# Ten retention query and key tiles moved to the seven-product pairs, with their rotation done per chunk on GpSimd

## What is computed

```python
proj = h @ w_in[l]
(c_q, c_kv, k_pe, gate_mla, q_ret, k_ret, v_ret, gate_ret,
 merge_mla, merge_ret) = jnp.split(proj, pts, axis=-1)
y_mla = mla_branch(...) * jax.nn.silu(gate_mla)            # 8 heads, causal softmax
y_ret = retention_branch(q_ret, k_ret, v_ret, positions, g_ret[l]) * jax.nn.silu(gate_ret)
merged = (jax.nn.sigmoid(merge_mla) * (y_mla @ w_proj_mla[l])
          + jax.nn.sigmoid(merge_ret) * (y_ret @ w_proj_ret[l]))
x = x + gate * (merged @ w_out[l])                         # then a final rmsnorm
```

```python
inner = (q k^T * decay) v        # within a chunk
cross = (q R) * xi               # with the state R of the chunks before
R = R * gamma_c + (k * zeta)^T v
```

## Time and profile before

| | |
|---|---|
| median of 3 runs | 1627.0 us (1626.59 to 1627.08) |
| the profiled execution: its time | 1629.6 us |
| its span, first to last instruction | 1627.8 us |
| PE busy | 1581.9 us, 97% of the span |
| DVE busy | 985.8 us, 61% |
| ACT busy | 579.9 us, 36% |
| POOL busy | 233.7 us, 14% |
| granted TensorE clock | 0.995 of full speed |
| instructions | 20108 |

### The profile page before, as it was taken

The page is one execution under the profiler, slowest core; times in us unless marked ns, Lnnn a source line. Parts: engine busy times, 40 slices in busy tenths (PEclk is TensorE's granted clock), DMA queues, the critical chain, the costliest instruction groups (busy, mean ns, idle before and its releaser), DMA issues.

```text
span 1627.8 us, 20108 instructions
## 1 busy us (share of the span) xinstructions
PE 1581.9 (97%) x7660; PEld 1320.8 (81%) x7660; DVE 985.8 (61%) x1576; ACT 579.9 (36%) x984; POOL 233.7 (14%) x180
## 2 busy tenths in 40 slices
PE   5999999999999999999999999999999999999998
PEld 4778888888888888888888878888788888888886
DVE  6984444444447957656665555657877775547544
ACT  5444333333334323332343333334543333213111
POOL 2232223323211212112000000001101000000000
PEclk9999999999999999999999999999999999999999
DMA  9132232233241576777655465537987877335322
GB/s 387 34 129 104 110 110 110 111 117 116 103 141 45 153 288 234 287 269 265 218 188 179 155 205 168 194 130 229 360 257 246 263 236 277 124 125 199 135 103 78
DMA packets 150991, 292.31 MB, mean 180 GB/s; under 512 B 10736, under 2 KB 91504, under 8 KB 142960
## 3 DMA queue, kind: packets, MB, share of 16 engines
q1 hardware_dynamic: 132816, 253.47, 45.0%
q10 hardware_dynamic: 13472, 20.78, 4.0%
q0 software_dynamic: 4608, 16.78, 2.6%
HBM read 187.71 MB, written 102.76 MB: 178 GB/s over the span
## 4 chain that ended last, share of the span: by engine, by line
PE 82%; DVE 10%; DMA 3%; ACT 3%; issue 1%; POOL 1%; SPq 0%; DVEq 0%; ACTq 0%
PE p_banks L2050 8%; PE p_banks L2008 8%; PE p_banks L2011 8%; PE p_banks L2010 8%; PE p_banks L1923 4%; PE p_banks L1925 4%; PE p_banks L1924 4%; PE p_banks L2082 4%; PE p_banks L2257 4%; PE p_banks L2256 4%; PE p_banks L2258 4%; PE p_banks L2315 2%; PE p_banks L2316 2%; PE p_banks L2317 2%; DMA w_raw<-in_w_dense 2%; PE p_banks L2149 2%
## 5 line engine op out<-in xcount | busy, mean ns | idle before, releaser
L1518 DVE TENSOR_TENSOR w_form<-w_pair,w_form 128x512 fp32r<-128x512 f32 x120 | 92.9, 776 | 101.8 <-ACT w_form L1172 100.5
L1172 ACT ACTIVATE w_form<-w_pair 128x512 fp32r<-128x512 f32 x120 | 75.6, 632 | 195.4 <-PE p_banks L2011 187.3
L519 ACT ACTIVATE w_hi<-w_raw 128x1024 fp32r<-128x1024 f32 (+3 forms) x79 | 70.1, 889 | 202.4 <-PE p_banks L2258 99.5
L1923 PE MATMUL p_banks<-h_hi,w_hi 128*128 128x512 f32 x304 | 118.6, 390 | 2.0 <-DVE w_lo L525 1.6
L1924 PE MATMUL p_banks<-h_lo,w_hi 128*128 128x512 f32 x304 | 118.4, 389 | 0.0
L1925 PE MATMUL p_banks<-h_hi,w_lo 128*128 128x512 f32 x304 | 118.3, 389 | 0.0
L525 DVE TENSOR_TENSOR w_lo<-w_raw,w_hi 128x1024 fp32r<-128x1024 f32 (+3 forms) x80 | 92.3, 1158 | 28.6 <-ACT w_hi L519 28.3
L1242 ACT ACTIVATE prob<-p_banks,neg_max 128x128 f32<-128x128 f32 (+3 forms) x64 | 47.5, 742 | 163.8 <-DVE neg_max L1621 163.8
L2258 PE MATMUL p_banks<-y_hi,w_lo 128*128 128x512 f32 x256 | 99.6, 389 | 0.0
L2257 PE MATMUL p_banks<-y_lo,w_hi 128*128 128x512 f32 x256 | 99.6, 389 | 0.0
L2256 PE MATMUL p_banks<-y_hi,w_hi 128*128 128x512 f32 x256 | 99.6, 389 | 0.0
(11 more groups left out here) (291 smaller groups left out, 4255.2 us busy)
## 6 DMA issues: line engine op xcount, KB each, us to landing
w_raw<-in_w_dense SPq DMA_DIRECT2D x45, 512.0 KB, 5.6
w_pair<-in_w_pairs SPq DMA_DIRECT2D x20, 1024.0 KB, 4.9
v_ret<-v_stage POOLq DMA_DIRECT2D x32, 512.0 KB, 4.1
qk_chunk<-qk_chunks SPq DMA_DIRECT2D x32, 512.0 KB, 4.4
v_chunk<-v_ret SPq DMA_DIRECT2D x32, 512.0 KB, 5.0
qk_chunks<-split_stage SPq DMA_DIRECT2D x28, 512.0 KB, 6.0
merge_t<-act_t SPq DMA_DIRECT2D x48, 256.0 KB, 3.4
act_t<-stage SPq DMA_DIRECT2D x40, 256.0 KB, 2.0
```

What stands on the lines that cost most here:

```text
L1518: nc.vector.tensor_tensor(self.form[f % FORM_SLOTS][:, 1, :], self.form_source(f), self.form[f % FORM_SLOTS][:, 0, :].bitcast(F32), ALU.su ...
L1923: nc.tensor.matmul(out, w_hi[:, slot, cut], x_hi[:, k, tok], start=(k == ks[0]), stop=False)
```

## The change

It does six things.

1. The first ten of the 16 retention query and key tiles (heads 0 and 1, and the queries of head 2) leave `SEQ` and form five more pairs (25 instead of 20). Six "x" tiles stay, three ahead of "q" 0 and three behind "v" 3; between them no "x" stands any more.
2. None of the 16 is rotated or split there. Their half tiles (pairs) or tiles (x) are copied by ACT and stored as plain float32 in chunk order, in pieces of 512 B. The scratch tensor `qk` has half its size.
3. In retention, a chunk's four raw tiles (256 KB) and its cosine and sine (128 KB, 512 B pieces) are loaded two chunks ahead into two slots. POOL rotates them with four instructions (`rotate_chunk`), ACT writes the high parts (`high_qk`) and DVE the low parts (`low_qk`). POOL's key sums go.
4. The norming of the latents is spread over the three first "x" tiles instead of six.
5. In attention, ACT's exp and DVE's reciprocal and scaling of a step stand ahead of the eviction of filled tiles instead of behind it.
6. In the last output tile, the left half's final scaling is done by ACT, beside DVE's of the right half, and its product with `g_final` is taken earlier.

```diff
+GATES = 16
+RAW, RAW_FIRST = 6, 3
...
-SEQ += [("x", n) for n in range(6)]
-SEQ += [("q", 0), ("q", 1), ("q", 2), ("q", 3), ("a", 0), ("b", 0), ("x", 6), ("q", 4), ("q", 5), ("x", 7),
-        ("q", 6), ("q", 7), ("a", 1), ("b", 1), ("x", 8), ("k", 0), ("k", 1), ("k", 2), ("k", 3), ("x", 9)]
+SEQ += [("x", n) for n in range(RAW_FIRST)]
+SEQ += [("q", 0), ("q", 1), ("q", 2), ("q", 3), ("a", 0), ("b", 0), ("q", 4), ("q", 5), ("q", 6), ("q", 7),
+        ("a", 1), ("b", 1), ("k", 0), ("k", 1), ("k", 2), ("k", 3)]
 for n in range(4):
-    SEQ += [("k", 4 + n), ("v", n)] + [("x", 10 + n)] * (n < 2)
-SEQ += [("x", n) for n in range(12, TURNS)]
+    SEQ += [("k", 4 + n), ("v", n)]
+SEQ += [("x", n) for n in range(RAW_FIRST, RAW)]
...
-PAIRS = ACT_TILES // 2
+GATE_PAIRS = ACT_TILES // 2
+PAIRS = GATE_PAIRS + (4 * H_RET - RAW) // 2
...
     def load_qk_chunk(self, sp, n):
-        if n >= 3:
-            sp.wait_ge(self.out_done, n - 2)
-        sp.dma_start(self.qk[:, n % 3, :, :].rearrange("p c n -> p (c n)").bitcast(F32), self.d["qk"][n // NT, n % NT])\
-            .then_inc(self.chunk_loaded[n % 3], 16)
+        if n >= 2:
+            sp.wait_ge(self.k_turned, n - 1)
+            sp.wait_ge(self.qk_lo_ready, n - 1)
+        h, m = divmod(n, NT)
+        sp.dma_start(self.qk_raw[:, n % 2, 0:4, :].rearrange("p c n -> p (c n)"), self.d["qk"][h, m])\
+            .then_inc(self.chunk_loaded[n % 2], 16)
+        sp.dma_start(self.qk_raw[:, n % 2, 4:6, :], self.d["ret_tables"].rearrange("a p n -> p a n")[:, :, m * P:(m + 1) * P])\
+            .then_inc(self.chunk_loaded[n % 2], 16)
...
         for n in range(CHUNK_STEPS):
+            if n + 2 < CHUNK_STEPS:
+                self.load_qk_chunk(sp, n + 2)
             if n + 3 < CHUNK_STEPS:
-                self.load_qk_chunk(sp, n + 3)
                 self.load_v_chunk(sp, n + 3)
...
+    def rotate_chunk(self, pool, n):
+
+        raw, late = self.qk_raw[:, n % 2, :, :], int(n >= 6)
+        by_sine = self.by_sine[late]
+        cos, sin = (raw[:, c:c + 1, :].broadcast_to([P, 4, P]) for c in (4, 5))
+        pool.wait_ge(self.chunk_loaded[n % 2], 32 * (n // 2 + 1))
...
+        if n:
+            pool.wait_ge(self.qk_step, 4 * n)
+        self.nc.gpsimd.tensor_tensor(by_sine[:, :, :], raw[:, 0:4, :], sin, ALU.mult).then_inc(self.qk_step, 1)
+        pool.wait_ge(self.qk_step, 4 * n + 1)
+        self.nc.gpsimd.tensor_tensor(raw[:, 0:4, :], raw[:, 0:4, :], cos, ALU.mult).then_inc(self.qk_step, 1)
+        pool.wait_ge(self.qk_step, 4 * n + 2)
+        self.nc.gpsimd.tensor_tensor(raw[:, 0:2, :], raw[:, 0:2, :], by_sine[:, 2:4, :], ALU.subtract).then_inc(self.qk_step, 1)
+        self.nc.gpsimd.tensor_tensor(raw[:, 2:4, :], raw[:, 2:4, :], by_sine[:, 0:2, :], ALU.add).then_inc(self.qk_step, 1)
...
+    def high_qk(self, act, n):
+        act.wait_ge(self.qk_step, 4 * n + 4)
+        if n >= 2:
+            act.wait_ge(self.out_done, n - 1)
+        self.nc.scalar.activation(self.qk[:, n % 2, 0:4, :], self.qk_raw[:, n % 2, 0:4, :], ACT.Copy).then_inc(self.qk_hi_ready, 1)
+
+    def low_qk(self, dve, n):
+        dve.wait_ge(self.qk_hi_ready, n + 1)
+        self.nc.vector.tensor_tensor(self.qk[:, n % 2, 4:8, :], self.qk_raw[:, n % 2, 0:4, :],
+                                     self.qk[:, n % 2, 0:4, :].bitcast(F32), ALU.subtract).then_inc(self.qk_lo_ready, 1)
...
             nc.vector.tensor_tensor(self.y_ret[:, s, :, :], p[:, 0, :].rearrange("p (a n) -> p a n", n=P),
                                     self.gate_chunk[:, n % 3, :, :], ALU.mult).then_inc(self.yr_done, 1)
+            if n + 2 < CHUNK_STEPS:
+                self.low_qk(dve, n + 2)
...
     def turn_keys(self, pe, n):
-        pe.wait_ge(self.k_summed, n + 1)
+        pe.wait_ge(self.qk_step, 4 * n + 4)
...
     def inner_scores(self, pe, n):
-        pe.wait_ge(self.chunk_loaded[n % 3], 16 * (n // 3 + 1))
+        pe.wait_ge(self.qk_lo_ready, n + 1)
```

262 lines of the change are left out of this document (141 added, 121 removed).

## The result

| | before | after |
|---|---|---|
| median | 1627.04 us (1626.59 to 1627.25, 4 executions) | 1679.70 us (1676.73 to 1680.08, 4 executions) |
| ratio, 95% interval | | 1.032 [1.0302, 1.0338] |
| span of the profiled execution | 1627.8 us | 1678.2 us |
| PE busy | 1581.9 us | 1587.8 us |
| POOL busy | 233.7 us | 322.9 us |

The change costs 52.7 us. The forecast was 1651, +24, with a range up to 1680: the sign and the place were right, the size was less than half of it.

The account below looks back on a forecast made before the run. PE, busy for 97% of the span, was taken to bound the kernel. 1629.6 - 13.6 + 38 + 3 - 3 - 0.6 = 1653.4; with the median 2.6 under the profiled execution, the forecast was 1651, range 1612 to 1680.

Parts of the forecast that it names:

- Fewer matmuls, -13.6: Pairs and sequence: five new pairs save 60 matmuls at 0.227 us each, all on the path, 13.6 us.
- the sequence, +3: Sequence: loads and stores of the unbroken "q" to "v" tiles make PE wait, +3 us, ends 0 and +12.
- The third rival: Sequence starves: loads and stores lag from k0 to v3, PE loses 12 us, total 1626, no difference; chance 0.05.
- Attention, -3: Attention: with exp ahead of evictions, PE's 4.3 us wait for exp shrinks, -3 us, ends 0 and -6.
- Retention, +38: Retention: the late-load rotation loop takes 17.6 us for two chunks, 8.8 a chunk against 7.54, times 30, +38 us.
- bn_stats to the end of `y_ret` (5.35 + 0.5): Retention loop: DVE's 5.35 us to the gated output, plus 0.5 us for POOL being in DVE's way, ends 0 and 2.6.
- The 0.15 taken off for chunks without a state: Retention loop: chunks at a head's end have no state, lowering the two-chunk sum from 17.75 to 17.6 us.
- The 0.5 us added to POOL's fourth instruction: Retention rotation: the fourth instruction stands straight behind another and takes longer, raising POOL's 4.1 us to 4.6.
- Hidden rotation: Retention: rival that the two-chunk loop takes no more than 15.1 us, total 1610, faster; chance 0.14.
- The case in which both DVE instructions wait at each chunk: Retention: rival that L1697 and L1702 each wait 1.30 us for POOL, 9.85 a chunk, +69 us, 1682; chance 0.10.
- Intervals of 8.5 to 9.2 us: Retention: sign that the forecast is right, starts of bn_stats 8.5 to 9.2 us apart; wrong if still near 7.6.
- both bounds: Retention loop: all low ends give 15.3 us, +4 us; all high ends over 10 a chunk, +80 and more.

Follow-up runs that it names:

- run 4: The changed kernel with ACT's and DVE's evictions of filled tiles put back ahead of exp, reciprocal and scaling in attention; 1678.3 us.
- run 2: The changed kernel with the move of the sine products, and POOL's wait for its last stores, at chunk 14 instead of chunk 6; 1673.0 us.
- runs 5 and 8: First: changed kernel, load issued before the `y_ret` wait, sine products moved at chunk 14, 1656.6 us. Second: the first plus ACT's high part earlier, 1641.3 us.

## Why the prediction was half right

**Fewer matmuls, -13.6, and the sequence, +3.** Together -10.6; measured -9.0. The pairs grew by 95.2 us, as forecast. The sequence lost 5.2 us to idle time of PE instead of 2.6, but only in part for the reason given. Its two long waits are these:

```profile
679.83 0.47 PE L1978 MATMUL p_banks<-c_hi,w_hi 128*128 128x512 f32 x1 [2.09 <-DVE split_stage L1441]
684.71 0.47 PE L1978 MATMUL p_banks<-c_hi,w_hi 128*128 128x512 f32 x1 [1.91 <-DVE split_stage L1441]
```

Before the first, DMA moved 102 GB/s (670 to 680 us). The split that PE waits for stands on DVE behind two others of 3.77 us together, and these behind POOL's rotation of the second "a" and "b" pair (670.93 to 675.87). Before the second, ACT waited 3.80 us for the landing of a query store; from 680 to 700 us DMA moved 419 GB/s. So one of the two waits is the backlog of stores that was forecast. The third rival, 12 us lost there, did not come.

**Attention, -3.** Measured +2.6. The wait for exp went from 4.3 to 0.8 us, as said, but run 4 shows that others took its place. The step that failed is "I take -3": a wait removed from PE was counted as time won. PE's waits in attention are 10.6 us in all against 8.4 before; the largest is now at the start of the filling, 4.4 us for `w_lo` (1.8 before). What makes that one longer was not tried.

**Retention, +38.** Measured +56.4, so this term holds 18 of the 29 us that were missing (attention 5.6, the sequence 1.6, start and end 1; and the last 2.3 are the step from the profiled execution to the median, 2.6 before and 0.3 now). At 1.26 us a chunk the forecast has 8.8 us for the first seven intervals and 30.2 for the other 24; they lost 21.8 and 34.6. So most of the miss lies in the first seven chunks. Two steps failed.

First, a term that was put at nothing without a reason: POOL's wait at chunk 6 for stores that it issued itself, 7 to 9 us (run 2). The change has it in `rotate_chunk`, `elif n == 6` with waits for the stores of the three staging slots. The prediction prices POOL's four instructions and names no wait of `rotate_chunk` but the one for the loads. The parts of it were in the trace of the kernel before: POOL issues these stores there too, and they took 6.9 us to landing (median of three in retention). Here the two took 8.0.

Second, the sizes of the loop over the other chunks. These are 27 loops of two chunks, without the two that hold the stall, in us:

| link | forecast | median | mean |
|---|---|---|---|
| bn_stats to the end of `y_ret` (5.35 + 0.5) | 5.85 | 6.00 | 5.93 |
| to POOL's start | 5.0 | 5.13 | 5.30 |
| rotation | 4.6 | 4.19 | 4.20 |
| high, low and handing over | 1.4 | 1.39 | 1.57 |
| to bn_stats | 0.9 | 1.18 | 1.15 |
| whole loop | 17.75 | 18.05 | 18.15 |

The links' own medians add up to 17.89, but the median of whole loops is 18.05 and their mean 18.15, because in many loops some link is late: a few loads come 1 us later, and at a few chunks ACT takes the rotation up late. A sum of typical durations misses that. Besides, the forecast had 0.25 us too little between the low part and bn_stats, and 0.4 too much for POOL. The 0.15 taken off for chunks without a state did not come: the loops that start at a head's end took 17.14, 17.46 and 19.46 us. 18.15 instead of 17.6 is 0.27 us a chunk, 8 us over 30. With the stall that is 15 to 17 of the 18 us.

The 0.5 us added to POOL's fourth instruction was wrong (0.74 like the third), and so was the reading of the earlier trace rows behind it: these rows show two durations, not what makes them differ. The interference with DVE came where the prediction put it, at L1746 and L1751, 0.3 and 0.4 us each in the mean, and at times for both: L1746 ends at 1310.36, 0.15 us after the POOL instruction that started before it (1310.21), and L1751 ends at 1311.72, 0.14 after the next (1311.58). There the Trainium skill (SBUF — State Buffer, section "Who interferes with whom"), by which the two exclude each other and the second is blocked until the first is done, agrees with the rows.

**The rivals.** Hidden rotation was out: the loop is 18.1, not 15.1. (Its 1610 also leaves out the +3 of the sequence.) The case in which both DVE instructions wait at each chunk, 1682, comes within 3 us of the measured time, but by another way: L1746 and L1751 took 0.59 and 0.66 us in the mean over 31 chunks, 0.3 and 0.4 more than alone and not 1.30 more each. A time that fits does not confirm its mechanism.

**What would show it.** Intervals of 8.5 to 9.2 us: their median is 9.1, but apart from the stall single ones swing from 7.5 to 11.2, and only 7 of the 31 lie in that band, since it is the loop of two chunks that is steady. DVE idle before L1312, released by ACT and that by POOL: 46.4 us in 25 waits. POOL released by the table load some 5 us after `y_ret`: 5.13. PE's waits for `out_n` and `inner_lo`: 33.8 us, just under the 35. The mechanism is as described.

**Beyond the forecast.** The prediction said that both bounds were slow "because the load starts so late". The load was only the first of three closures of the loop: SP's wait, ACT's order, POOL's length. The loop had some 45 us to give, 29 chunks of 9.07 against 7.54; opening it at SP alone gave 11.9 of them. Order and places together (runs 5 and 8) take the change from 1679.7 to 1641.3. What is left is POOL's two products, 14.2 us, and that is as much as the 13.6 us that the pairs save. None of the versions that keep the rotation beat the kernel before.
